# Pairwise last expert iteration, full-precision token gather, four gather banks and later row loads in a two-layer diffusion backbone

## What is computed

```python
def hierarchical_moe(h, rg_w, rg_b, re_w, re_b, w_gate, w_up, w_down):
    ...                       # top-1 group of 4, top-2 experts of 8: `combine` (tokens x 32 weights)
    hid = silu(einsum('bsd,edf->bsef', h, w_gate)) * einsum('bsd,edf->bsef', h, w_up)
    hid = hid * combine[..., None]
    return einsum('bsef,efd->bsd', hid, w_down)

# per layer, after the mixers:
y  = hierarchical_moe(modulate(xp, sh2, sc2), *moe_w)
xp = layer_norm(DEEPNORM_ALPHA * xp + g2 * y, ln2_g[l], ln2_b[l])
```

## Time and profile before

| | us |
|---|---|
| median of 3 runs (lowest, highest) | 1087.92 (1087.81, 1088.95) |
| the profiled execution: its time, and its span from first to last instruction | 1086.85, 1085.1 |
| PE busy | 967.4 (89% of the span) |
| PE weight loads | 590.2 |
| DVE, ACT, POOL busy | 326.5, 230.6, 39.6 |
| one `high` (line 1175), one `low` (line 1557), mean | 0.69, 0.75 |
| one scatter for one request, in the chain of waits | 1.13 |
| mean granted TensorE clock | 0.965 of full speed |

### The profile page before, as it was taken

The page is one execution under the profiler, slowest core; times in us unless marked ns, Lnnn a source line. Parts: engine busy times, 40 slices in busy tenths (PEclk is TensorE's granted clock), DMA queues, the critical chain, the costliest instruction groups (busy, mean ns, idle before and its releaser), DMA issues.

```text
span 1085.1 us, 15639 instructions
## 1 busy us (share of the span) xinstructions
PE 967.4 (89%) x6820; PEld 590.2 (54%) x6820; DVE 326.5 (30%) x744; ACT 230.6 (21%) x475; POOL 39.6 (4%) x60
## 2 busy tenths in 40 slices
PE   3999899998899898978879998999998989897875
PEld 1887758777743333334248876687884333332421
DVE  2112323222851312111170132331276231211215
ACT  2102314200251312111121132241014231211211
POOL 1100000010000000000010000000001000000000
PEclk9899999999999999998989999999999999999998
DMA  9938854586439999999875426766442999999970
GB/s 381 409 141 348 335 224 155 219 318 274 160 132 422 389 427 429 429 427 423 374 304 219 161 63 239 316 272 209 182 174 82 413 428 429 429 430 429 422 310 39
DMA packets 38526, 324.60 MB, mean 299 GB/s; under 512 B 4920, under 2 KB 5048, under 8 KB 9392
## 3 DMA queue, kind: packets, MB, share of 16 engines
q1 hardware_dynamic: 33696, 308.82, 69.6%
q0 software_dynamic: 4320, 13.28, 3.5%
q10 hardware_dynamic: 432, 1.39, 0.3%
HBM read 321.05 MB, written 2.42 MB: 298 GB/s over the span
## 4 chain that ended last, share of the span: by engine, by line
PE 75%; DMA 10%; DVE 6%; ACT 5%; issue 3%; SPq 1%; DVEq 0%; ACTq 0%
PE ps L768 13%; PE ps L666 9%; PE ps L817 8%; PE ps L692 6%; PE ps L872 5%; PE ps L944 5%; PE ps L958 5%; PE ps L781 5%; DMA expert_gate_up<-in_w_gu 4%; DMA expert_down<-in_w_dn 3%; PE ps L595 3%; PE ps L725 2%; PE ps L616 2%; DMA dense<-in_w_ada 2%; PE ps L827 2%
## 5 line engine op out<-in xcount | busy, mean ns | idle before, releaser
L768 PE MATMUL ps<-expert_gate_up,gathered_prompt 128*32 128x512 f32 x768 | 172.4, 603 | 5.0 <-ACT gathered_sample L1143 2.3
L768 PE MATMUL ps<-expert_gate_up,gathered_sample 128*32 128x512 f32 x768 | 172.4, 603 | 0.0
L817 PE MATMUL ps<-expert_down,hiddenT 128*32 128x512 f32 x1024 | 117.5, 602 | 11.8 <-ACT gathered_sample L1143 4.5
L666 PE MATMUL ps<-hT,dense 128*128 128x256 f32 x512 | 115.9, 385 | 0.0
L768 PEld LDWEIGHTS ps<-expert_gate_up,gathered_prompt 128*32 128x32 f32 x768 | 49.8, 111 | 115.6 <-issue 112.9
L666 PEld LDWEIGHTS ps<-hT,dense 128*128 128x128 f32 x512 | 97.4, 192 | 16.1 <-issue 2.8
L1557 DVE SCALAR_TENSOR_TENSOR y_lo<-ps,slot_weight,y_hi 128x512 fp32r<-128x512 f32 x64 | 48.1, 751 | 105.7 <-ACT y_hi L1175 105.6
L817 PEld LDWEIGHTS ps<-expert_down,hiddenT 128*32 128x32 f32 x1024 | 32.0, 110 | 82.8 <-issue 57.4
L1540 DVE TENSOR_TENSOR hidden<-hidden,ps 128x256 f32<-128x256 f32 x32 | 13.4, 420 | 194.0 <-ACT hidden L1159 194.0
L692 PE MATMUL ps<-dense,hT 128*128 128x256 f32 (+1 forms) x320 | 69.3, 381 | 1.7 <-ACT hT L1100 1.7
L692 PEld LDWEIGHTS ps<-dense,hT 128*128 128x128 f32 x320 | 60.6, 201 | 10.4 <-ACT hT L1100 2.5
(11 more groups left out here) (217 smaller groups left out, 1110.1 us busy)
## 6 DMA issues: line engine op xcount, KB each, us to landing
expert_gate_up<-in_w_gu SPq DMA_DIRECT2D x64, 2048.0 KB, 17.6
expert_down<-in_w_dn SPq DMA_DIRECT2D x64, 1024.0 KB, 12.9
dense<-in_w_ada SPq DMA_DIRECT2D x48, 1024.0 KB, 9.1
dense<-in_w_in SPq DMA_DIRECT2D x28, 1024.0 KB, 9.3
dense<-in_w_o SPq DMA_DIRECT2D x8, 1024.0 KB, 6.3
dense<-in_w_out SPq DMA_DIRECT2D x8, 1024.0 KB, 5.1
dense<-in_w_c SPq DMA_DIRECT2D x4, 1024.0 KB, 24.6
gate<-ada_rows POOLq DMA_DIRECT2D x4, 1024.0 KB, 8.5
```

The lines of the kernel that those rows point to most:

```text
L666: last = mm(b[:, m * 256:(m + 1) * 256], w[:, k, m * P:(m + 1) * P], hT[:, k, :], start=(k == 0), stop=(k == KD - 1))
L768: last = mm(ps[r0:r0 + 32, q, :], xg[s][:, k, at_:at_ + CAP], w_gu[(i * EPI + 2 * q + j) % SLOTS][:, k, :], start=(k == 0), stop=(k == KD ...
L817: last = mm(ps[32 * e:32 * e + 32, banks[c], :], h, w_dn[(i * EPI + e) % SLOTS][:, f, c * 512:(c + 1) * 512], start=(f == 0), stop=(f == 1 ...
```

## The change

1. The gather multiplies `xh2` itself by a float32 `sel`, one product instead of two. `h_hi`, `h_lo`, ACT's two copies and POOL's two subtractions a layer are gone, with their waits.
2. `gather_pair` takes four banks, 2, 3, 0 and 1. Bank 0 holds the transposed hidden values and bank 1 the transposed `sel`, so k = 2 and k = 3 wait until these were read; the waits on the bank's own readers begin at k = 4.
3. Iteration 7 goes pairwise like iterations 1 to 6. PE's order is: q = 0, scatter of iteration 6 for s = 0, q = 1, scatter for s = 1, `turn_pairs`, `down` for s = 0, first half of `down` for s = 1, scatter for s = 0, second half, scatter for s = 1. DVE's order moves `low` of s = 1 ahead of most of the row work for s = 0. `expert_pass` follows.
4. The rows for the end of the layer are issued by SP, behind the last down load and ahead of the next layer's dense loads.

```diff
@@ -54,6 +54,7 @@
+GATHER_BANK = (2, 3, 0, 1)
@@ -212,10 +213,8 @@
-        h_hi = arena("h_hi", 16, [P, 2, D], F32R)
-        h_lo = arena("h_lo", 24, [P, 2, D], F32R)
 ...
-        sel = arena("select", 48, [P, 2, 2, CHUNK], F32R)
+        sel = arena("select", 48, [P, 2, 2, CHUNK])
@@ -295,7 +294,7 @@
-        x1_ready, xh2_ready, hi_ready, lo_ready = sem("x1_ready"), sem("x_hat2_ready"), sem("hi_ready"), sem("lo_ready")
+        x1_ready, xh2_ready = sem("x1_ready"), sem("x_hat2_ready")
@@ -305,7 +304,7 @@
-                     "hidT_filled": ITERS + 2, "hidT_copied": ITERS + 2, "y_filled": 4 * ITERS,
+                     "hidT_filled": ITERS + 1, "hidT_copied": ITERS + 1, "y_filled": 4 * ITERS,
@@ -361,7 +360,7 @@
-            return 2 * i + 2 if i in (0, ITERS - 1) else 2 * i + (e % EPI) // 2 + 1
+            return 2 * i + 2 if i == 0 else 2 * i + (e % EPI) // 2 + 1
@@ -369,6 +368,15 @@
+
+        def load_rows(eng, l, part, out, s):
+
+            src = dram(io["ada"], (l * 2 * ADA + part) * D, [[0, P], [ADA * D, 2], [1, D]])
+            eng.dma_start(out[:, :, :], src).then_inc(s, 16)
+
+        def load_ln(eng, l, name, out, s):
+            for j, n in enumerate((name + "_g", name + "_b")):
+                eng.dma_start(out[:, j, :], dram(io[n], l * D, [[0, P], [1, D]])).then_inc(s, 16)
@@ -472,6 +480,10 @@
+                sp.wait_ge(*reached(M[l], "xg_filled", 2 * KD + (PAIRS - 1) * KD))
+                sp.wait_ge(ada_stored, 32 * (2 * l + 2))
+                load_rows(sp, l, 5, g2, post2_in)
+                load_ln(sp, l, "ln2", ln2, post2_in)
@@ -487,14 +499,7 @@
-            def load_rows(l, part, out, s):
-
-                src = dram(io["ada"], (l * 2 * ADA + part) * D, [[0, P], [ADA * D, 2], [1, D]])
-                pool.dma_start(out[:, :, :], src).then_inc(s, 16)
-
-            def load_ln(l, name, out, s):
-                for j, n in enumerate((name + "_g", name + "_b")):
-                    pool.dma_start(out[:, j, :], dram(io[n], l * D, [[0, P], [1, D]])).then_inc(s, 16)
+
@@ -536,21 +541,13 @@
-                load_rows(l, 2, g1, post1_in)
-                load_ln(l, "ln1", ln1, post1_in)
+                load_rows(pool, l, 2, g1, post1_in)
+                load_ln(pool, l, "ln1", ln1, post1_in)
 ...
-                for s in range(2):
-                    pool.wait_ge(hi_ready, 2 * l + s + 1)
-                    nc.gpsimd.tensor_tensor(h_lo[:, s, :], xh2[:, s, :], h_hi[:, s, :].bitcast(F32),
-                                            ALU.subtract).then_inc(lo_ready, 1)
 ...
-                pool.wait_ge(*reached(m, "xg_filled", 2 * KD + (PAIRS - 1) * KD))
-                pool.wait_ge(ada_stored, 32 * (2 * l + 2))
-                load_rows(l, 5, g2, post2_in)
-                load_ln(l, "ln2", ln2, post2_in)
@@ -721,9 +718,8 @@
-                    for hp, part in enumerate((h_hi, h_lo)):
-                        last = mm(ps[:, bank, at_ * CHUNK:(at_ + 1) * CHUNK], part[:, s, k * P:(k + 1) * P],
-                                  sel[:, n % 2, s, :], start=(hp == 0), stop=(hp == 1))
+                    last = mm(ps[:, bank, at_ * CHUNK:(at_ + 1) * CHUNK], xh2[:, s, k * P:(k + 1) * P],
+                              sel[:, n % 2, s, :], start=True, stop=True)
@@ -733,12 +729,16 @@
-            def gather_pair(w, n, evacs):
+            def gather_pair(w, n, evacs, turns, copies):
 ...
-                    if k >= 2:
-                        pe.wait_ge(*reached(w, ("xg_act", "xg_dve")[k % 2], evacs + k // 2))
-                    gather(w, n, k, 2 + k % 2, (0, 1))
+                    if k == 2 and turns is not None:
+                        pe.wait_ge(*reached(w, "hidT_copied", turns))
+                    if k == 3 and copies is not None:
+                        pe.wait_ge(*reached(w, "selT_copied", copies))
+                    if k >= 4:
+                        pe.wait_ge(*reached(w, ("xg_act", "xg_dve")[k % 2], evacs + k // 2 - 1))
+                    gather(w, n, k, GATHER_BANK[k % 4], (0, 1))
@@ -749,7 +749,7 @@
-                    picked = sel[:, i // 2 % 2, s, at_:at_ + P].bitcast(F32)
+                    picked = sel[:, i // 2 % 2, s, at_:at_ + P]
@@ -799,13 +799,13 @@
-            def down(w, r, g, i, s, banks, paired, turns):
+            def down(w, r, g, i, s, banks, paired, turns, halves=(0, 1)):
 ...
-                for c in range(2):
+                for c in halves:
@@ -833,7 +833,7 @@
-                    gather_pair(w, n, r * (4 * PAIRS) + 4 * n)
+                    gather_pair(w, n, r * (4 * PAIRS) + 4 * n, None, None)
@@ -977,8 +977,7 @@
-                pe.wait_ge(hi_ready, 2 * l + 1)
-                pe.wait_ge(lo_ready, 2 * l + 1)
+                pe.wait_ge(xh2_ready, 2 * l + 1)
@@ -989,8 +988,7 @@
-                pe.wait_ge(hi_ready, 2 * l + 2)
-                pe.wait_ge(lo_ready, 2 * l + 2)
+                pe.wait_ge(xh2_ready, 2 * l + 2)
@@ -1030,7 +1028,7 @@
-                        gather_pair(m, n, 4 * n + 4)
+                        gather_pair(m, n, 4 * n + 4, i + 2, i + 3)
@@ -1046,22 +1044,19 @@
-                        gather_pair(m, n, 4 * n + 4)
+                        gather_pair(m, n, 4 * n + 4, i + 2, i + 3)
 ...
-                gate_up_request(m, i, 0, 0, range(0, 8))
-                for s in range(2):
-                    scatter(m, i - 1, i - 1, s, False)
-                turn_request(m, i, 0, 0)
-                down(m, None, i, i, 0, (2, 3), False, ITERS + 1)
-                gate_up_request(m, i, 1, 1, range(0, 4))
+                for q in range(2):
+                    gate_up_pair(m, None, i, q)
+                    scatter(m, i - 1, i - 1, q, False)
+                turn_pairs(m, i)
+                down(m, None, i, i, 0, (2, 3), True, i + 2)
+                down(m, None, i, i, 1, (2, 3), True, i + 2, (0,))
 ...
-                gate_up_request(m, i, 1, 1, range(4, 8))
-                turn_request(m, i, 1, 1)
-                pe.wait_ge(*reached(m, "lo_done", 4 * i + 2))
-                down(m, None, i, i, 1, (2, 3), False, ITERS + 2)
+                down(m, None, i, i, 1, (2, 3), True, i + 2, (1,))
@@ -1152,7 +1147,7 @@
-                    spread(w, n, k, 2, (0, 1))
+                    spread(w, n, k, GATHER_BANK[k % 4], (0, 1))
@@ -1252,16 +1247,12 @@
-                act.wait_ge(xh2_ready, 2 * l + 1)
-                actf(h_hi[:, 0, :], xh2[:, 0, :], ACT.Copy).then_inc(hi_ready, 1)
 ...
-                act.wait_ge(xh2_ready, 2 * l + 2)
-                actf(h_hi[:, 1, :], xh2[:, 1, :], ACT.Copy).then_inc(hi_ready, 1)
@@ -1294,15 +1285,13 @@
-                silu(m, i, 0, 0)
-                turned_request(m, 0, 0, ITERS + 1)
-                for c in range(2):
-                    high(m, i, i, 0, c, 2 + c, i + 2)
-                silu(m, i, 1, 1)
-                turned_request(m, 1, 1, ITERS + 2)
+                for q in range(2):
+                    silu(m, i, q, q)
+                turned_pairs(m, i + 2)
+                for s in range(2):
+                    for c in range(2):
+                        high(m, i, i, s, c, 2 + c, i + 2)
 ...
-                for c in range(2):
-                    high(m, i, i, 1, c, 2 + c, i + 2)
@@ -1533,7 +1522,7 @@
-                    spread(w, k, 3, (0, 1))
+                    spread(w, k, GATHER_BANK[k % 4], (0, 1))
@@ -1783,17 +1772,17 @@
-                hidden_product(m, i, 0, 0)
+                for q in range(2):
+                    hidden_product(m, i, q, q)
 ...
+                low(m, i, i, 1, 0, 2)
 ...
+                low(m, i, i, 1, 1, 3)
 ...
-                hidden_product(m, i, 1, 1)
 ...
-                low(m, i, i, 1, 0, 2)
 ...
-                low(m, i, i, 1, 1, 3)
```

## The result

| | before | after |
|---|---|---|
| median, us (lowest, highest) | 1088.04 (1087.81, 1088.95) | 1079.20 (1078.38, 1079.88) |
| ratio of after to before, 95% interval | | 0.9925 (0.9911 to 0.9938) |
| profiled execution: its time, its span | 1086.85, 1085.1 | 1079.88, 1077.9 |
| PE busy, POOL busy | 967.4, 39.6 | 972.1, 26.4 |
| mean granted clock | 0.965 | 0.974 |

The change gains 0.75%, 8 us. The forecast was 1087.0, with a range of 1083.5 to 1090.0: too slow by 8 us, and the result lies outside the range.

The account below looks back on a forecast made before the run. Bound by the memory stream until iteration 5's down, then PE, then DVE's row work. Layer 0 +0.6 and layer 1 -0.95, with the median 1.07 above the profiled execution, gave 1087.0 us; 80% range 1083.5 to 1090.0.

Parts of the forecast that it names:

- Bounds of the kernel: Expert part: the memory stream bounds up to iteration 5's down projection, then PE's chain, then DVE's row work.
- First gathers: Ahead of the stream's start: full-precision products cost the sample request +1.07 us a layer, the prompt request +0.3.
- The split: First stage, POOL's subtraction and ACT's copy gone: gains 0.27 us in layer 1, nothing in layer 0.
- Pair gathers: Two ahead of iteration 5: 8.2 us each instead of 7.9 at the high clock, +0.3 us a layer taken.
- Third gather: Behind the branch, PE starting at the low clock: about 10.4 us, +0.7 in layer 0, +1.55 in layer 1.
- Gate and up of iteration 6: Layer 0, behind the third gather: a gather without holes keeps the clock high, -1.2 us.
- Rows: Moved out of the stream: last gate/up load lands about 3 us earlier, but this doesn't count with the pairwise form.
- pairwise form: Last iteration, from the end of down of iteration 6: -0.6 us in layer 0, -4.5 in layer 1.
- (d): Rival: DVE was the limit ahead of the router, so its 1.7 us count in both layers; 1083.9 us, chance 0.04.
- (a): Rival: the stream swallows the early gathers' cost, as the ring of five slots sets iteration 5; 1083.9 us, chance 0.23.
- (b): Rival: the clock stays low behind the branch, third gather and gate/up of iteration 6 slow; 1091.9 us, chance 0.15.
- (c): Rival: loads of experts 28 and 29 land after down, so the pairwise form doesn't start early; 1089.5 us, chance 0.08.

Follow-up runs that it names:

- e7: The change with the reduced two-part gather put back, over four banks: 1072.82 us, ratio 0.9864 to the kernel before.
- e1: The kernel before with only the full-precision gather, still over two banks: 1088.56 us, ratio 1.0018.
- e13: e10 plus 14 unused transposes in PE's hole of the prompt request's first gather, written to a work bank: 1068.41 us, ratio 0.9852 to the kernel before.
- e10: The kernel before with four banks and the rows behind the last load only; reduced gather, old last iteration: 1070.54 us, ratio 0.9859.
- e8: The change with ACT's copies and POOL's subtractions put back, their output unused: 1080.76 us, ratio 0.9934 to the kernel before.
- e14: The kernel before with only the four banks: 1083.69 us, ratio 0.9975.
- e3: The kernel before with only the pairwise last iteration: 1082.02 us, ratio 0.9947.
- e4: The kernel before with only the rows issued by SP behind the last load; old last iteration: 1080.27 us, ratio 0.9936.
- e9: The kernel before, unchanged, profiled again: gate and up of iteration 6 in layer 0 took 13.97 us, not 15.67.
- e6: The change with the rows left on POOL's queue in the middle of the loads: 1079.02 us, ratio 0.9934 to the kernel before.
- e11: e10 with the register load of the number of rounds put ahead of the last step before the branch: 1073.42 us, ratio 0.9869 to the kernel before.

## Why the prediction missed

**Bounds of the kernel:** right. The stream sets the start of iteration 5's down: in layer 0, from the end of the sample request's first gather to there, kernels with pair gathers of 5.2, 7.9 and 8.3 us (e7, before, after) take 154.4, 155.2 and 155.3 us. At 9.84 us (e1) PE sets it, with 158.3. The wait for the last gate/up load, for which the prediction gave a size only in layer 1, also sets layer 0's tail before.

**First gathers, "+1.4" and "+1.1":** the step that failed. They are +0.15 and -0.8. The products cost about what was said (+1.26 for the sample request, +1.07 forecast). What was left out is the other end: the sparse gather had let the clock fall, and the steps behind it were paid at half clock. The prediction used this very argument for the third gather and not for the first. In e13 the whole first stage is 0.5 us shorter than before in layer 0 and 1.25 in layer 1; in layer 0 e10, the kernel without the filler, was itself slower than before, by 0.5 us. The prompt request's +0.3 didn't come: from the start of its gather to the transposes behind it, both kernels take 5.29 us in both layers.

**The split, "0 and -0.27":** too small; e8 gives -0.6 and -0.8. PE's bracketed idle time was read as the whole effect. But DVE's delay also reaches PE through steps that touch without a bracket (from the output's transposes to the router layer 0 took 4.56 us, and takes 4.33 now), and ACT's second copy holds PE up by 0.3 us once PE runs at full clock. These shares close the account: for layer 0 clock 0.5, split 0.6, prompt request 0.3, less 0.2 for the dearer products, is 1.25 us; for layer 1 it is 1.25 + 0.5 + 0.3 - 0.2, about 1.9. Together they are 3.1 of the 7.8 us by which the forecast missed, the largest share that the edits explain.

**Pair gathers, +0.3 and 8.2 us:** right, 8.3 us, and +0.2 and +0.15, though the sum as written, 6.9 + 1.14, gives 8.05: the blocks took 7.15. **Third gather, 10.4:** right, 10.54 and 9.93. But its price was counted against a gather over two banks. With the reduced gather the four banks take it to 7.2 and 6.6 us (e7; 7.0 and 7.2 in e14), so that in the change the full precision costs 6.7 us that the sum never saw, because the two parts were costed as one.

**Gate and up of iteration 6, -1.2:** right in mechanism, and -1.7 between these two profiles, with -0.6 for the tail behind it as forecast. Over two banks with the reduced gather 3 of 8 such stretches ran at the low clock (15.6 us; before, e3, e4), with four banks or full precision none of 24. But the kernel before lost nothing by the low clock: e9 shows the 1.7 us swallowed by the wait for a load. The two terms hold only together; against e9 they are 0 and -3.4.

**Rows, nothing; pairwise form, -4.5 and -0.6:** right as a pair (e6, and -5.8 for e3). The working "brings the last gate/up load forward by at most 4.9 us" already pointed at e4's result: without the pairwise form the rows' move alone gives 7 us by the ratio. That the two parts are substitutes, and each nearly useless beside the other, was not drawn from it.

**Rivals:** (d) was right in part: of DVE's 1.7 us, 0.3 and 0.5 us reach PE (e8). (a) holds for the pair gathers alone: e7's first two are 6 us shorter than the change's together, and from its first gathers to iteration 5 it takes only 0.9 us less in layer 0. The first gathers' own shift isn't swallowed: from there on before and after take 155.2 and 155.3 us. (b) didn't happen: the granted clock (0.70 between 488 and 490, 0.84 between 1004 and 1006) puts the low stretches of the third gathers at 4.6 and 3.4 us, and gate and up behind them ran at full clock. (c) didn't happen.

**The range** ended at 1083.5 because it took the cases one at a time. Here the first stages' 1.25 and 1.9 us came together with 0.7 more behind layer 0's branch. The rest of the miss isn't shown to be an effect of the change: -1.8 and -0.4 us in dense parts that no edit touches, and the 1.75 us by which the profiled execution stood differently to its median. Runs of the kernel before spread over 1084 to 1091 us.

## What to carry to other kernels

Cost each part of a combined change alone and beside each of the others: two parts may remove the same wait (here the pairwise form and the rows' place, 5.8 and 7 us alone by the ratios, nothing that can be told beside each other), and one part may cost what another would have gained (the full precision, 6.7 us of the four banks' gain). Where PE waits in holes ahead of a dense stretch, look at the granted clock behind the holes: a sparse step's price includes the half clock after it, and filling the hole can be cheaper than making the step denser. Profile the kernel before twice, and compare profiles stage by stage: a stretch that differs between a kernel's own profiles is no term of a sum, and a part that no edit touches can differ by 3 us.

## What the runs showed of the hardware

- TensorE's granted clock was 1.2 GHz instead of 2.4 for some 3 us (layer 1, windows of 0.70, 0.50 and then 0.95) behind a step in which it had been idle for 2.04 us between short bursts. With 14 throwaway transposes in that hole, 1.7 us busy and 0.5 us idle left, it stayed at 2.4 (e13).
- A part of the code that no edit touches, layer 0's dense part, ended 2.4 us earlier to 2.1 us later than in the first profile, over 15 others. Layer 1's took 242.2 to 245.2 us, with a granted clock of 1.00 or 0.97 between 60 and 120 us behind its start.
- Around a branch that isn't taken PE was idle for 5.7 to 6.5 us in both layers, DVE for 5.4 to 6.4 us in layer 0 but for 0.47 us in layer 1. An earlier register load (e11) took 1.2 and 0.8 us off PE's part and 1.1 off DVE's; a gain in the kernel's time couldn't be told.
- A POOL subtraction of 128x1024 stretched one DVE instruction from 0.42 to 1.91 us, but what follows on PE began only 0.3 (layer 0) and 0.5 us (layer 1) later (e8).
